# Two float32 projections of a streaming encoder's cross attention, written as split products

## The chip, the cores and the metric

The kernel runs on one core of a Trainium2 chip. The metric is the device time of one execution in microseconds, as the median over several runs. TensorE (PE in the profile) multiplies, VectorE (DVE) and ScalarE (ACT) do the elementwise work, GpSimd (POOL) and SyncE (SP) issue transfers.

## What is computed

One inference step of a two-layer encoder for 512 prompt frames and 32 sample frames, 544 columns in all, with 1024 features. Each layer has a mixer sub-layer with three branches, a cross attention into 256 memory tokens, and a SwiGLU FFN, each between a norm before and a norm behind. The part that matters here:

```python
def _rmsnorm(x, g):
    x32 = x.astype(jnp.float32)
    y = x32 * lax.rsqrt(jnp.mean(x32 * x32, axis=-1, keepdims=True) + RMS_EPS)
    return (y * g.astype(jnp.float32)).astype(x.dtype)
...
def _cross_attention(h, mem_k, mem_v, w_xq, w_xo):
    b, t, _ = h.shape
    q = (h @ w_xq).reshape(b, t, XATTN_HEADS, XATTN_HEAD_DIM)
    s = jnp.einsum('bqhd,bkhd->bhqk', q, mem_k).astype(jnp.float32) * XATTN_HEAD_DIM ** -0.5
    p = jax.nn.softmax(s, axis=-1)
    o = jnp.einsum('bhqk,bkhd->bqhd', p.astype(mem_v.dtype), mem_v).reshape(b, t, XATTN_W)
    return o @ w_xo
...
    x = x + _rmsnorm(y, norm_mix_post)
    x = x + _rmsnorm(_cross_attention(_rmsnorm(x, norm_x_pre), mem_k, mem_v, w_xq, w_xo), norm_x_post)
    x = x + _rmsnorm(_swiglu(_rmsnorm(x, norm_ffn_pre), w_ffn_in, w_ffn_out), norm_ffn_post)
```

`w_xq` is 1024 x 512, `w_xo` is 512 x 1024, all in float32.

## The kernel before

The residual `xT` and the normalised input `hT` stay on chip, features on the partitions, as 8 tiles of 128 x 544. A dense product makes one output tile of 128 features at a time: for each of its 8 (or 4) input tiles, one weight tile of 128 x 128 stands against two halves of 272 columns. There are two ways to do it:

- `dense` (line 716) multiplies in float32 straight from the weight ring. One matmul of it shows as two records in the profile.
- `dense_split` (line 726) takes weight and input each as a high and a low part in the type fp32r and sums three products: high x high, high x low, low x high. VectorE splits the weights in `split_unit` (line 1867): a cast of the ring slot into `WHI` (line 1865 of the helper `take_high`) and a subtraction into `WLO` (line 1875). Both have two places, taken in turn, so a tile can be split once the tile two before it has been multiplied. The input is split once, in `prenorm_split` (line 1834): two `scalar_tensor_tensor` for a pair of tiles, a drain, a cast, a drain, a subtraction that adds one to `x_split`.

Before the change all dense products of the layers are split but those of the memory keys and values (`w_xkv`, line 1258), the queries (`w_xq`) and the attention output (`w_xo`), both of them line 722.

The weights come through `ring`, four slots of 8 x 128 columns, filled by SyncE in the order of use (`unit`, line 447). Each load waits until the slot's last user is done: for a split tile that is its split (`split_done`), for a float32 tile the product itself (`tile_done`). Two ring slots serve two memory tiles, so the slots of the first two `w_xq` tiles come free when the sixth of the eight memory tiles is done:

```python
                for j in range(8):
                    unit("w_xkv", 0, 8, P * j, tiles(G_MEM + 2 * (j // 2) + 2))
                for j in range(4):
                    unit("w_xq", 0, 8, P * j, tiles(G_XQ + j + 1))
```

Nothing is scheduled by a planner: each engine has its program written out in order, and semaphores tie them. On VectorE the order around the change is: the last evacuations of the mixer's output product; `postnorm` (adds the mixer's result to `xT`, which lets ScalarE square it and TensorE sum it); a wait for `rstd_ready`, the reciprocal norm; `prenorm` (line 1828, writes `hT`); one scaled copy for each query tile; the barrier `phase_end`; attention; the sum of the squares of the output tiles (`add_square`, line 1819), which TensorE's `norm_added` takes; the first two FFN splits; the next norm. TensorE goes meanwhile through the memory products, the query product, attention (scores, transposed probabilities, values for 17 tiles, four heads), and the output product. In attention VectorE takes the maximum, the reciprocal and the scaling of each tile, and at four points (`x_evac`, after tiles 8, 12, 16 and at the end) it copies one head's 128 x 512 result from PSUM into `OX`; the 32 sample columns are one small copy at tile 4. ScalarE does the exponentials and copies the transposed probabilities.

## Time and profile before

| | |
|---|---|
| median of 3 runs | 2880.22 us (2878.37 to 2882.38) |
| the profiled execution | 2874.14 us, span 2872.3 us |
| granted TensorE clock, mean | 0.991 |
| TensorE busy | 2750.8 us (96%) |
| VectorE busy | 1611.0 us (56%) |
| ScalarE busy | 753.7 us (26%) |
| GpSimd busy | 244.2 us (9%) |
| DMA engines' share taken by the main queue | 28.7% |

Busy time is the time in which an engine had an instruction under way; it does not say that the end depended on it. The chain of work that ended last does: it is followed back from the last instruction, at each step to what released it. A timeline has one line for a run of like instructions, with the start, the length, and in brackets how long the engine was idle before it and what ended that. The granted clock is 1.00 at 2.4 GHz and 0.50 at 1.2 GHz.

### The profile page before, as it was taken

What the parts mean: (1) busy time and instruction counts of PE and PEld (TensorE: products, weight loads), DVE (VectorE), ACT (ScalarE), POOL (GpSimd) and SP (SyncE); (2) the same over time, 40 slices, a digit from 0 to 9 for tenths busy, and PEclk for the clock granted to TensorE, in tenths of its full rate; (3) what the DMA queues carried; (4) which work ended last, traced back from release to release, by engine and by line L of the source; (5) the groups of instructions that cost most, each with busy time, mean ns of one, the idle gap of its engine ahead of it and who ended that gap; (6) DMA issues with size and microseconds to landing.
All of it is one profiled execution on the core that took longest, in us unless ns stands there. A gap on an engine that the chain in (4) does not pass through costs nothing.

```text
span 2872.3 us, 63037 instructions
## 1 busy us (share of the span) xinstructions
PE 2750.8 (96%) x26472; PEld 2571.1 (90%) x26472; DVE 1611.0 (56%) x2967; ACT 753.7 (26%) x1803; POOL 244.2 (9%) x423
## 2 busy tenths in 40 slices
PE   7999999999999989999989999999999998999998
PEld 6877889999999789999988778899999996999997
DVE  5444665666664266664374455556666533766633
ACT  1143343333332330000112433433223324200001
POOL 1221112000000100000001211110000000000000
PEclk9999999999999999999999999999999999999999
DMA  4453436222263133333234434452224532233231
GB/s 136 127 144 105 144 107 170 72 72 65 82 173 100 46 89 89 89 87 88 77 90 132 120 111 139 103 160 72 72 68 115 153 92 73 71 89 89 85 88 58
DMA packets 420762, 290.26 MB, mean 101 GB/s; under 512 B 38544, under 2 KB 386352, under 8 KB 420352
## 3 DMA queue, kind: packets, MB, share of 16 engines
q1 hardware_dynamic: 398496, 228.64, 28.7%
q0 software_dynamic: 21984, 57.59, 6.3%
q8 instruction: 210, 3.44, 0.5%
q14 instruction: 72, 0.59, 0.1%
HBM read 232.12 MB, written 54.07 MB: 100 GB/s over the span
## 4 chain that ended last, share of the span: by engine, by line
PE 80%; DVE 8%; ACT 3%; DVEq 3%; DMA 2%; issue 2%; ACTq 0%; SPq 0%
PE PS L744 35%; PE PS L813 10%; PE PS L1116 8%; PE PS L1049 7%; PE PS L722 4%; PE PS L1258 2%; DMA U<-gate_scratch 2%; ACT U L1373 1%; PE PS L859 1%; PE PS L1090 1%; ACT U L1376 1%; PE PS L895 1%; PE PS L763 1%; PE PS L974 1%; PE PS L1194 1%
## 5 line engine op out<-in xcount | busy, mean ns | idle before, releaser
L744 PE MATMUL PS<-U_r,WHI 128*128 128x272 f32 x2656 | 474.4, 289 | 12.5 <-DVEq L2285 9.0
L1376 ACT COPY U<-PS 128x272 f32<-128x272 f32 (+9 forms) x782 | 273.1, 373 | 728.3 <-PE PS L1116 139.8
L1865 DVE CAST WHI<-ring 128x1024 fp32r<-128x1024 f32 (+1 forms) x240 | 164.1, 684 | 473.3 <-PE PS L744 365.3
L744 PEld LDWEIGHTS PS<-U_r,WHI 128*128 128x128 f32 x2656 | 386.1, 188 | 18.1 <-DVEq L2285 13.2
L744 PE MATMUL PS<-brT_r,WHI 128*128 128x272 f32 x1728 | 357.3, 288 | 1.4 <-DVEq L1876 1.4
L744 PE MATMUL PS<-U_r,WLO 128*128 128x272 f32 x1696 | 350.0, 288 | 0.0
L744 PE MATMUL PS<-hT_r,WHI 128*128 128x272 f32 x1696 | 349.7, 288 | 0.0
L1875 DVE TENSOR_TENSOR WLO<-ring,WHI 128x1024 fp32r<-128x1024 f32 (+1 forms) x240 | 289.7, 1207 | 19.4 <-issue 1.3
L744 PE MATMUL PS<-brT_r,WLO 128*128 128x272 f32 x1344 | 278.2, 288 | 0.0
L744 PEld LDWEIGHTS PS<-brT_r,WHI 128*128 128x128 f32 x1728 | 271.5, 188 | 2.2 <-DVEq L1876 2.2
L813 PE MATMUL PS<-U_r,WHI 128*128 128x272 f32 x832 | 261.6, 314 | 12.2 <-ACT U L1376 12.0
L744 PEld LDWEIGHTS PS<-hT_r,WHI 128*128 128x128 f32 x1696 | 266.5, 189 | 0.0
L744 PEld LDWEIGHTS PS<-U_r,WLO 128*128 128x128 f32 x1696 | 265.6, 188 | 0.0
L813 PE MATMUL PS<-U_r,WLO 128*128 128x272 f32 x832 | 242.1, 291 | 0.0
L813 PE MATMUL PS<-hT_r,WHI 128*128 128x272 f32 x832 | 241.0, 290 | 0.0
L1049 PE MATMUL PS<-U_r,WHI 128*128 128x272 f32 x768 | 229.7, 299 | 2.8 <-DVEq L2080 2.4
L1049 PE MATMUL PS<-U_r,WLO 128*128 128x272 f32 x768 | 221.8, 289 | 0.0
L1049 PE MATMUL PS<-hT_r,WHI 128*128 128x272 f32 x768 | 220.9, 288 | 0.0
L1116 PE MATMUL PS<-U 64*64 64x64 f32 (+1 forms) x5184 | 213.2, 238 | 0.0
L744 PEld LDWEIGHTS PS<-brT_r,WLO 128*128 128x128 f32 x1344 | 209.8, 189 | 0.0
L1116 PEld LDWEIGHTS PS<-U 64*64 64x64 f32 x5184 | 207.2, 134 | 1.3
L813 PEld LDWEIGHTS PS<-U_r,WHI 128*128 128x128 f32 x832 | 158.7, 191 | 31.5 <-issue 15.0
(336 smaller groups left out, 4291.5 us busy)
## 6 DMA issues: line engine op xcount, KB each, us to landing
ring<-in_w_in_dram SPq DMA_DIRECT2D x126, 512.0 KB, 4.3
ring<-in_w_ffn_in_dram SPq DMA_DIRECT2D x88, 512.0 KB, 3.8
ring<-in_w_ffn_out_dram SPq DMA_DIRECT2D x32, 448.0 KB, 3.7
proj_scratch<-U POOLq DMA_DIRECT2D x104, 136.0 KB, 2.1
U<-proj_scratch SPq DMA_DIRECT2D x48, 272.0 KB, 4.2
ring<-in_w_branch_dram SPq DMA_DIRECT2D x48, 256.0 KB, 3.2
gate_scratch<-U POOLq DMA_DIRECT2D x88, 136.0 KB, 3.2
U<-gate_scratch SPq DMA_DIRECT2D x44, 272.0 KB, 2.9
```

The costliest lines, as they stand in the source:

```text
L722: ins = mm(PS[0:width, 2 * q + h, 0:HT], ring[:, n % RING, k, 0:width], rhs(k, h), start=(k == 0), stop=(k == kn - 1))
L744: ins = mm(PS[:, 2 * q + h, 0:HT], w, half(x, h), start=(first and k == 0 and n == 0), stop=(last and k == kn - 1 and n == len(terms) - 1))
L763: ins = mm(PS[:, 2 * j + h, 0:HT], w, half(x, h), start=(k == 0 and n == 0), stop=(k == KM - 1 and n == 2))
L813: ins = mm(PS[:, 7, 0:HT], w, half(x, h), start=(k == 0 and i == 0), stop=(k == 7 and i == 2))
L859: mm(PS[:, b, 0:n], q, FK[it % 2][0:66, h, 0:n], start=True, stop=False)
L895: ins = mm(PS[o, 6, i * P:(i + 1) * P], FVT[it % 2][:, h, t, :], pt[:, t * P:(t + 1) * P], start=(t == 0), stop=(t == i))
L1049: ins = mm(PS[:, 6 + h, 0:HT], w, half(x, h), start=(k == 0 and i == 0), stop=(k == 7 and i == 2))
L1116: ins = mm(PS[r, bank, cols], w_c[r], x_c[r], start=(n == 0), stop=(n == len(pairs) - 1))
L1258: ins = mm(PS[:, 2 + n % 4, u * P:(u + 1) * P], MNT[:, k, t * P:(t + 1) * P], ring[:, (U_MEM + 2 * s + u) % RING, k, :], start=(k == 0), s ...
L1376: return act.copy(out, in_)
L1865: copy(hi, src)
L1875: tt(lo, w, hi.bitcast(F32), ALU.subtract)
```

## The change

The query and the output product become split products. In detail:

- The tables of split tiles get four entries for `w_xq` (`V_XQ`, 95) and eight for `w_xo` (`V_XO`, 99); the FFN's numbers move up by 12. The ring's order and its unit numbers stay.
- `prenorm` of the query's input becomes `prenorm_split`, with the high part in a new buffer `XH` and the low part in `hT`'s place. TensorE starts its first query tile pair by pair as `x_split` rises, where it waited for all of `hT` before.
- VectorE splits the query's first two weight tiles between `postnorm` and `prenorm_split`, the third and the fourth behind the first and the second product; the first two tiles of `w_xo` at the start of attention, the others in the output product.
- `x_evac` and the copy of the sample columns each become a cast into `OXH` and, after a drain, a subtraction into `OXL`.
- The additions of squares and the first two FFN splits now lie between the output product's splits, one tile behind the other.
- SyncE's loads for slots that `w_xq` and `w_xo` have used wait for the split and not for the product.

```diff
-V_LATE, V_GATE, V_BR, V_OUT, V_FFI, V_FFO = 13, 39, 63, 87, 95, 139
+V_LATE, V_GATE, V_BR, V_OUT, V_XQ, V_XO, V_FFI, V_FFO = 13, 39, 63, 87, 95, 99, 107, 151
...
@@ -52,17 +52,17 @@
 IN_PAIR = (0, 1, 3, 2, 0, 1, 2, 0, 1, 2, 0, 2, 1)
 IN_ROT = (4, 4, 4, 4, 4, 4, 3, 3, 3, 3, 3, 2, 4)
 SPLITS = V_FFO + 8 * len(FFO_SPLIT)
-X_SPLITS = 4 + 6 + 8
+X_SPLITS = 4 + 6 + 4 + 8
 
 
 def unit_of(v):
 
-    return v if v < V_FFI else v + U_FFI - V_FFI
+    return v if v < V_XQ else v + U_XQ - V_XQ
 
 
 def depth_of(v):
 
-    if V_BR <= v < V_OUT:
+    if V_BR <= v < V_OUT or V_XO <= v < V_FFI:
         return 4
     return FFO_SPLIT[(v - V_FFO) % 3] if v >= V_FFO else 8
 
@@ -329,6 +329,7 @@
         BH = cv(12, T, of=UR)
         MNT = cv(KM, N_MEM)
         SQ1 = cv(KM, T)
+        XH = carver(2 * KM * T + T + 6 * T + 12 * T + KM * N_MEM)(KM, T, of=UR)
         YH = carver(0)(KM, T, of=UR)
 
         cv = carver(KM * T + T)
@@ -339,6 +340,8 @@
         OX = cv(X_HEADS, T)
         XP, XPT = cv(3, N_MEM), cv(2, 2 * P)
         XST = cv(3, 4)
+        OXH = cv(X_HEADS, T, of=UR)
+        OXL = carver(KM * T + T + 2 * 512 * 4 + 2 * X_HEADS * N_MEM + X_HEADS * T)(X_HEADS, T, of=UR)
 
         cv = carver(0)
         GH, GL = cv(KF, T, of=UR), cv(KF, T, of=UR)
@@ -615,9 +618,9 @@
                 for j in range(8):
                     unit("w_xkv", 0, 8, P * j, tiles(G_MEM + 2 * (j // 2) + 2))
                 for j in range(4):
-                    unit("w_xq", 0, 8, P * j, tiles(G_XQ + j + 1))
+                    unit("w_xq", 0, 8, P * j, split(V_XQ + j))
                 for j in range(8):
-                    unit("w_xo", 0, 4, P * j, tiles(G_XO + j + 1))
+                    unit("w_xo", 0, 4, P * j, split(V_XO + j))
                 for j in range(11):
                     for m in range(4):
                         unit("w_ffn_in", 0, 8, (m // 2) * FFN + 256 * j + P * (m % 2), split(V_FFI + 4 * j + m))
@@ -1263,9 +1266,9 @@
                     if s == 1:
                         group_sums(l, 2, 0)
                         group_sums(l, 2, KM // 2)
-                pe.wait_ge(h_ready, l * 24 + 16)
                 for n in range(N_XQ):
-                    dense(l, G_XQ + n, n % 4, U_XQ + n, 8, of_h, rot=3)
+                    dense_split(l, G_XQ + n, n % 4, V_XQ + n, lambda k: (XH[:, k, :], hTR[:, k, :]), rot=3,
+                                need=10 if n == 0 else None)
                 phase_end(pe, l, 2)
                 pe.wait_ge(xa_loaded, (l + 1) * 32)
 
@@ -1325,7 +1328,7 @@
                         x_values(k - 3)
                 pe.wait_ge(xa_evac, l * 5 + 5)
                 for n in range(N_XO):
-                    dense(l, G_XO + n, n % 3, U_XO + n, 4, lambda k, h: half(OX[:, k, :], h), rot=3)
+                    dense_split(l, G_XO + n, n % 3, V_XO + n, lambda k: (OXH[:, k, :], OXL[:, k, :]), rot=3)
                 norm_added(l, 3)
 
 
@@ -1336,7 +1339,7 @@
                 def of_f(k):
                     return HF[:, k, :], hTR[:, k, :]
 
-                dense_first(l, G_FFI, V_FFI, of_f, 10, sums=4)
+                dense_first(l, G_FFI, V_FFI, of_f, 14, sums=4)
                 sums_spread(l, 4)
                 ffn_in(0, 2, 1)
                 pe.wait_ge(rstd_ready, l * 6 + 5)
@@ -2322,16 +2325,25 @@
                         if 1 <= n - 2 <= KM - 3:
                             add_square(l, 1, n - 2)
                 postnorm(l, 1, "norm_mix_post")
-                prenorm(l, 2, "norm_x_pre")
+                split_unit(l, V_XQ)
+                split_unit(l, V_XQ + 1)
+                prenorm_split(l, 2, "norm_x_pre", XH)
                 for n in range(N_XQ):
                     tile(l, G_XQ + n)
+                    if n < N_XQ - 2:
+                        split_unit(l, V_XQ + n + 2)
                     ts(half(QX[:, n, :], 1), PS[:, 2 * (n % 4) + 1, 0:HT], X_DIM ** -0.5, None, ALU.mult) \
                         .then_inc(tile_freed_dve, 1)
                 phase_end(dve, l, 2)
+                split_unit(l, V_XO)
+                split_unit(l, V_XO + 1)
 
                 def x_evac(h):
                     dve.wait_ge(xa_out, l * 5 + h + 2)
-                    copy(OX[:, h, 0:SEQ], PS[:, x_bank(h), :]).then_inc(xa_evac, 1)
+                    take_high(OXH[:, h, 0:SEQ], PS[:, x_bank(h), :])
+                    dve.drain()
+                    tt(OXL[:, h, 0:SEQ], PS[:, x_bank(h), :], OXH[:, h, 0:SEQ].bitcast(F32), ALU.subtract) \
+                        .then_inc(xa_evac, 1)
 
                 for k in range(N_XT + 1):
                     if k < N_XT:
@@ -2347,16 +2359,19 @@
                             .then_inc(xa_norm, 1)
                     if k == 4:
                         dve.wait_ge(xa_out, l * 5 + 1)
-                        copy(OX[:, :, SEQ:T], PS[:, 7, 0:4 * DEC_SEQ].rearrange("p (h n) -> p h n", h=4)) \
-                            .then_inc(xa_evac, 1)
+                        rows = PS[:, 7, 0:4 * DEC_SEQ].rearrange("p (h n) -> p h n", h=4)
+                        take_high(OXH[:, :, SEQ:T], rows)
+                        dve.drain()
+                        tt(OXL[:, :, SEQ:T], rows, OXH[:, :, SEQ:T].bitcast(F32), ALU.subtract).then_inc(xa_evac, 1)
                     if k in (8, 12, 16):
                         x_evac((k - 8) // 4)
                 x_evac(3)
                 dve.sem_inc(tile_freed_dve, N_XO)
-                for a in range(1, KM - 2):
-                    add_square(l, 3, a)
-                split_unit(l, V_FFI)
-                split_unit(l, V_FFI + 1)
+                for n in range(N_XO):
+                    tile(l, G_XO + n)
+                    split_unit(l, V_XO + n + 2)
+                    if 1 <= n - 1 <= KM - 3:
+                        add_square(l, 3, n - 1)
                 dve.wait_ge(rstd_ready, l * 6 + 4)
 
                 def updated(b):
```

How VectorE's instructions move, between the post-norm and attention (in `prenorm` and its successor; `hT` is the normalised input, `VT` the gains, `U` the pool in which `XH` lies, `U_r` and `hT_r` the same memory as fp32r). Before:

```order
L1858 SCALAR_TENSOR_TENSOR hT<-hT,VT,U 128x544 x2
L1855 TENSOR_TENSOR xT<-xT,hT 128x544 x2
L1832 SCALAR_TENSOR_TENSOR hT<-xT,VT,U 128x544 [waits rstd_ready]
L1832 SCALAR_TENSOR_TENSOR hT<-xT,VT,U 128x544 x7
L2328 TENSOR_SCALAR U<-PS 128x272 [waits tile_done] x4
L2339 TENSOR_REDUCE U<-PS 128x1 [waits xa_scores,phase_ended]
```

and with the change:

```order
L1861 SCALAR_TENSOR_TENSOR hT<-hT,VT,U 128x544 x2
L1858 TENSOR_TENSOR xT<-xT,hT 128x544 x2
L1868 CAST WHI<-ring 128x1024 [waits slot_loaded3]
L1878 TENSOR_TENSOR WLO<-ring,WHI 128x1024
L1868 CAST WHI<-ring 128x1024 [waits slot_loaded0]
L1878 TENSOR_TENSOR WLO<-ring,WHI 128x1024
L1842 SCALAR_TENSOR_TENSOR hT<-xT,VT,U 128x544 [waits rstd_ready]
L1842 SCALAR_TENSOR_TENSOR hT<-xT,VT,U 128x544
L1868 CAST U_r<-hT 128x1088
L1847 TENSOR_TENSOR hT_r<-hT,U_r 128x1088
L1842 SCALAR_TENSOR_TENSOR hT<-xT,VT,U 128x544 x2
L1868 CAST U_r<-hT 128x1088
```

Two splits, each behind the arrival of its ring slot, now stand between the last instruction of the post-norm and the first that waits for the reciprocal norm.

The second place is VectorE from the end of attention to the norm behind it. Before:

```order
L2344 RECIPROCAL U<-U 128x1 [waits xa_exp]
L2346 TENSOR_SCALAR U<-U 128x256
L2334 COPY U<-PS 128x512 [waits xa_out]
L1822 TENSOR_TENSOR U<-U 128x544 [waits sq_act] x5
L1865 CAST WHI<-ring 128x1024 [waits slot_loaded3]
L1875 TENSOR_TENSOR WLO<-ring,WHI 128x1024
L1865 CAST WHI<-ring 128x1024 [waits slot_loaded0]
L1875 TENSOR_TENSOR WLO<-ring,WHI 128x1024
L2363 SCALAR_TENSOR_TENSOR hT<-hT,VT,U 128x544 [waits rstd_ready]
```

and with the change (the splits of `w_xo` are the ones of 512 columns; five more of them, with four additions of squares, stand between the two pieces shown):

```order
L2356 RECIPROCAL U<-U 128x1 [waits xa_exp]
L2358 TENSOR_SCALAR U<-U 128x256
L1868 CAST U_r<-PS 128x512 [waits xa_out]
L2345 TENSOR_TENSOR U_r<-PS,U_r 128x512
L1868 CAST WHI<-ring 128x512 [waits slot_loaded1,tile_done]
L1878 TENSOR_TENSOR WLO<-ring,WHI 128x512
```

```order
L1825 TENSOR_TENSOR U<-U 128x544 [waits sq_act]
L1868 CAST WHI<-ring 128x1024 [waits slot_loaded3,tile_done]
L1878 TENSOR_TENSOR WLO<-ring,WHI 128x1024
L1825 TENSOR_TENSOR U<-U 128x544 [waits sq_act]
L1868 CAST WHI<-ring 128x1024 [waits slot_loaded0,tile_done]
L1878 TENSOR_TENSOR WLO<-ring,WHI 128x1024
L2378 SCALAR_TENSOR_TENSOR hT<-hT,VT,U 128x544 [waits rstd_ready]
```

The copy of a head is now two instructions, and the additions of squares, which had the output product to themselves, each stand behind a split that waits for its tile.

## Rows read from the trace of the kernel before

**Rows 1.** The page, the chain that ended last: by engine, then by line.

```profile
PE 80%; DVE 8%; ACT 3%; DVEq 3%; DMA 2%; issue 2%; ACTq 0%; SPq 0%
PE PS L744 35%; PE PS L813 10%; PE PS L1116 8%; PE PS L1049 7%; PE PS L722 4%; PE PS L1258 2%; DMA U<-gate_scratch 2%; ACT U L1373 1%; PE PS L859 1%; PE PS L1090 1%; ACT U L1376 1%; PE PS L895 1%; PE PS L763 1%; PE PS L974 1%; PE PS L1194 1%
```

**Rows 2.** Timeline of PE, first layer: start us, us, engine, line, op, out<-in, count.

```profile
913.63 10.88 PE L1258 MATMUL PS<-ring,U 128*128 128x128 f32 x96
924.35 29.50 PE L722 MATMUL PS<-hT,ring 128*128 128x272 f32 x128
985.63 29.60 PE L722 MATMUL PS<-U,ring 128*128 128x272 f32 x128 [0.78 <-DVE U L2334]
```

**Rows 3.** Timeline of DVE, same stretch; idle before and releaser in brackets.

```profile
915.49 5.66 DVE L1832 SCALAR_TENSOR_TENSOR hT<-xT,VT,U 128x544 f32<-128x544 f32 x8 [9.56 <-ACTq L1411]
931.89 0.44 DVE L2328 TENSOR_SCALAR U<-PS 128x272 f32<-128x272 f32 x1 [10.75 <-PE PS L722]
953.89 0.44 DVE L2328 TENSOR_SCALAR U<-PS 128x272 f32<-128x272 f32 x1 [6.89 <-PE PS L722]
...
959.14 0.95 DVE L2339 TENSOR_REDUCE U<-PS 128x1 f32<-128x256 f32 x2 [4.81 <-PE PS L1288]
```

**Rows 4.** SP's timeline in both layers; then landing of the first and second load.

```profile
917.40 8.14 SPq L458 DMA_DIRECT2D ring<-in_w_xq_dram  x4
...
2337.62 8.14 SPq L458 DMA_DIRECT2D ring<-in_w_xq_dram  x4
...
DMA to landing us min/median/max: 3.8/3.8/3.8
...
DMA to landing us min/median/max: 5.0/5.0/5.0
```

**Rows 5.** Timeline of DVE: two weight tiles of depth 8 split back to back.

```profile
1010.04 0.69 DVE L1865 CAST WHI<-ring 128x1024 fp32r<-128x1024 f32 x1
1012.14 0.69 DVE L1865 CAST WHI<-ring 128x1024 fp32r<-128x1024 f32 x1
```

**Rows 6.** Timeline of DVE: the normalised input split in pairs, start of layer 2.

```profile
1458.74 0.73 DVE L1865 CAST U_r<-hT 128x1088 fp32r<-128x1088 f32 x1
1460.75 1.47 DVE L1839 SCALAR_TENSOR_TENSOR hT<-xT,VT,U 128x544 f32<-128x544 f32 x2
1462.32 0.73 DVE L1865 CAST U_r<-hT 128x1088 fp32r<-128x1088 f32 x1
1466.27 0.69 DVE L1865 CAST WHI<-ring 128x1024 fp32r<-128x1024 f32 x1 [1.86 <-PE PS L763]
```

**Rows 7.** Timeline of PE: the matmuls that wait for the last pair there.

```profile
1464.46 0.52 PE L763 MATMUL PS<-U_r,WHI 128*128 128x272 f32 x2
```

**Rows 8.** Timeline of DVE: two splits that each wait for a split-product tile.

```profile
1092.29 0.69 DVE L1865 CAST WHI<-ring 128x1024 fp32r<-128x1024 f32 x1 [3.12 <-PE PS L744]
1098.30 0.69 DVE L1865 CAST WHI<-ring 128x1024 fp32r<-128x1024 f32 x1 [3.11 <-PE PS L744]
```

**Rows 9.** Windows of PE: stretch, us, busy (x), granted clock, DMA share, GB/s.

```profile
1023.60:1026.60 3.00, 2.98 (x13) 0.50 0.02 5
1432.00:1436.70 4.70, 0.14 (x2) 0.95 0.00 0
1436.70:1440.00 3.30, 3.25 (x8) 0.55 0.00 0
2444.20:2449.70 5.50, 5.50 (x24) 0.50 0.01 3
```

**Rows 10.** The chain of waits through the first layer's attention tiles.

```profile
971.16 0.60 DVE U L2334
984.89 0.70 DVE U L2334
```

**Rows 11.** Groups of DVE instructions by form, 600 to 860 us: busy, mean ns.

```profile
L2284 DVE TENSOR_TENSOR WLO<-ring,WHI 128x512 fp32r<-128x512 f32 x22 | 15.2, 690 | 13.6 <-ACT WHI L1376 13.6
L2226 DVE COPY U<-PS 128x384 f32<-128x384 f32 x6 | 3.3, 558 | 4.7 <-PE PS L1116 4.7
```

## The prediction

> **What bounds the kernel now.** I read the chain that ended last first: TensorE holds 80% of it, and most lines in it are split products that the change does not touch; the plain float32 products of line 722 are 4% and the memory products of line 1258 are 2% [rows 1]. So what the change can move is small, and it is read from the one stretch between the mixer and the FFN, which both layers pass alike. The timelines of TensorE and VectorE there show four things. The memory products run until 924.35 and the query product follows without a gap; it takes 29.50 us, and the output product takes 29.60 us [rows 2]. VectorE idles 9.56 us for the reciprocal norm once the post-norm is over, from 905.93, and normalises from 915.49 for 5.66 us, so it is done before TensorE wants it [rows 3]. In between, attention goes tile by tile through all three engines. Last, the timeline of the load queue: the first two `w_xq` tiles are issued only at 917.40 [rows 4]. They go into ring slots that the memory products of `w_xkv` hold until their sixth tile is done, and that is the row to keep in mind.
>
> **Cheaper matmuls (the gain).** A float32 tile of 16 matmuls takes (953.89 - 931.89) / 3 = 7.33 us [rows 3]. A split tile of the same size, 48 matmuls, takes 1098.30 - 1092.29 = 6.01 us [rows 8], or 0.125 us a matmul. The output product has eight tiles of half that depth: 8 x (7.33 - 6.01) / 2 = 5.3 us less. The query product has four tiles; the last three save 3 x 1.32 = 4.0 us. The first is told below.
>
> **A rule on this term.** In the rows a split tile costs 6.01 / 7.33 = 0.82 of a float32 tile [rows 3, 8]. The Trainium skill (FP8 and Floating Point Precision, TensorE Precision Notes) says that true FP32 takes four passes through the array. By that three products at a pass each would cost 0.75; the trace does not agree with that ratio here, and what it would make of the time is a rival below.
>
> **The two splits ahead of the pre-norm (the price).** VectorE works in order. It now reaches the split of the first query tile at 905.93, and that split waits for its ring slot. The loads are issued at 917.40, and from issue to landing the first takes 3.8 us and the second, issued right behind, 5.0 us [rows 4]. Nothing in the change releases those slots sooner: they wait for memory tiles whose code is the same. So the first split starts at 917.40 + 3.8 = 921.2. One split takes 1012.14 - 1010.04 = 2.10 us [rows 5], and the second load has landed by about 922.9, before the first split ends at 923.3. Both end at 925.4. The wait for the reciprocal norm ended at 915.49, so the pre-norm starts 9.9 us late, and the idle time that was to hide the splits has passed before they can begin. Queued behind the waiting split on VectorE are the pre-norm and the halves of the input; TensorE waits for these.
>
> **The pre-norm itself is longer.** The start of the second layer shows the same helper: one pair of tiles comes every 1462.32 - 1458.74 = 3.58 us, and from the start of the last pair's first instruction to the matmuls that wait for it are 1464.46 - 1460.75 = 3.71 us [rows 6, 7]. Here the four pairs release TensorE at 929.1, 932.7, 936.3 and 925.4 + 3 x 3.58 + 3.71 = 939.9. A tile's share of a pair is 12 matmuls, 1.5 us, so TensorE is starved throughout. From the release of the last pair until VectorE sees the first tile done are 1466.27 - 1464.46 = 1.8 us there, and as many matmuls lie in between [rows 6, 7]. So the first query tile is seen done at 941.7 instead of 931.89 [rows 3]: 9.8 us later. With the 4.0 us saved behind it, the query product ends **5.8 us later** in each layer. The two other query splits (2.1 us each) lie beside tiles of 6.01 us and cost nothing.
>
> **The clock.** TensorE will be idle from 924.35 to 929.1, 4.75 us, and after that works 1.5 us of each 3.58. The trace has such a case: of the 4.70 us before 1436.7 it was busy 0.14 us, and in the stretch behind it the granted clock was 0.55; behind the waits ahead of the FFN it is 0.50 (the lower of its two levels, 1.2 GHz) for 3.0 us in one layer and for 5.5 us in the other, at 3.00 / 13 = 0.23 us a matmul [rows 9]. A slow clock costs nothing while pairs are awaited (12 x 0.23 = 2.8 us, under 3.58), but it does once the last pair is there. I take 12 x (0.23 - 0.125) = 1.3 us a layer; the bounds are 0 and half of the longest stretch, 2.75 us. The Trainium skill (TensorE: Matmul & The Clock Gate, HAM oscillation) describes short bursts of matmuls between waits that each start on the throttled clock. By that the upper bound would be nearer.
>
> **Attention.** `x_evac` becomes a cast from PSUM and a subtraction from PSUM with a drain between. The copy it replaces takes 0.60 us of the chain [rows 10], and the cast should match it. The subtraction: 0.69 us for 128x512 between SBUF tiles, and a PSUM copy of 384 columns takes 0.56, so PSUM is no dearer [rows 11]. With the drain I take 0.77 us for each of the four heads. The chain holds this copy at heads 0 and 1 and at head 3 (the first and the last of the three: [rows 10]), so there it counts in full, 2.3 us. At head 2 it delays the last normalisation, which has a few tenths of slack: 0.5 us. The small one for the 32 sample rows (about 0.35 us more) has slack in the next tile. Sum **2.8 us**; bounds 0.75 (only the last head counts, the engines catch up elsewhere) and 3.4 (all of it). The two output splits of depth 4 come first in this stage, while VectorE idles 4.81 us until its first score at 959.14 [rows 3]; a cast of 0.42 and a subtraction of 0.69 with drains are 1.3 us, twice that is 2.6, so they are hidden. In the output product VectorE has for each tile a split (1.3) and an addition of 544 columns (by the 0.69 for 512 some 0.8 with its drain), 2.1 us beside 3.0; with the depth-8 split of the FFN's first tile it is 2.10 + 0.8 = 2.9 beside 3.0, so I give 0.1 us to the sum of squares behind the last tile. The FFN splits were hidden before and are now.
>
> **The sum.** For each layer: +5.8 (query) + 1.3 (clock) + 2.8 (attention) - 5.3 (output) + 0.1 = +4.7 us, and twice that is **+9.4 us**. Against the profiled execution (2874.14 us, span 2872.3) that is 2883.5. The median of the runs shown is 6.1 us above that execution, so the forecast for the median is 2880.2 + 9.4 = **2889.6 us**, 0.33% slower. About 0.2%, 5.8 us, is what a measurement of this kernel can tell from no change.
>
> **Rivals.** *Attention absorbs it and the clock stays up:* 5.8 + 0.75 - 5.3 = +1.3 a layer, +2.5 us, 2882.7, no change to be told. For it speaks that the three engines each have idle time in a tile; against it, that the copies stand on the chain by name. Chance 0.17.
> *The splits are hidden after all (faster):* the two loads are in the ring before VectorE has to start splitting, at 915.49 - 4.2 = 911.3. Then the last pair is released at 915.5 + 14.5 = 930.0, the first tile is seen at 931.8, as before, and a layer changes by -4.0 + 2.8 - 5.3 = -6.5 us, -13 us in all, 2867. It decides at 911.3 for the second load's landing; the row says 922.9 and the issue itself is at 917.40 [rows 4], so it needs slots that come free 11 us sooner. Chance 0.04.
> *A split matmul costs a quarter of a float32 one:* a split tile is then 7.33 x 0.75 = 5.5 us, which takes 2.0 us more from the output product and 1.5 us more from the three query tiles, 3.5 a layer: +2.4 us in all, 2882.6. The 6.01 us of a split tile [rows 8] is TensorE back to back, each with VectorE waiting 3.1 us for it, so 0.03. That rule is the one of the Trainium skill named above (FP8 and Floating Point Precision).
> *Every bound at its dear end:* +5.8 + 2.75 + 3.4 + 0.3 - 5.3 = +6.95 a layer, +13.9 us, 2894.1; chance 0.16, the same sign as the forecast. The forecast itself has 0.60. That the change does not do what it says I leave at nothing: the order of instructions shows every edit in place.
>
> **How the numbers follow.** The range takes in the second rival's neighbours on the low side and the dear end on the high side, with two microseconds for the measurement at each: 2881 to 2896. Slower by over 0.2%: the forecast and the dear end, 0.76, less a little for the forecast without a slow clock (+6.8 us, close to the limit): 0.74. Within 0.2%: 0.17 + 0.03 + 0.02 = 0.22. Faster: 0.04.
>
> **What would show it.** In the profile of the changed kernel VectorE's first query split starts near 921 with some 15 us of idle before it, put down to the load; the pre-norm starts near 925.4; TensorE is idle some 4.7 us between the memory and the query products; the first query tile ends near 941.7 and the last near 959.7; the granted clock between 929 and 943 is under 1. From the first score to the output product attention is 2.8 us longer, and the output product takes 24.2 us. A first query split that starts before 916 would make the prediction wrong, and so would attention that grows by less than a microsecond, or an output product above 27 us.

## The result, and the profile after

The change makes the kernel slower: 2887.40 us as the median of 12 runs (2883.54 to 2893.13), against 2877.67 us of the kernel before in as many (2872.56 to 2882.72). The ratio is 1.0035, with a 95% interval of 1.0025 to 1.0045, or +9.7 us. The forecast was +9.4 us; its 2889.6 us stood on the 2880.22 us of the three runs known then.

The execution that was profiled is the slowest of the twelve: 2893.13 us, span 2891.2, mean granted clock 0.984, against 2874.14, 2872.3 and 0.991 of the profile before. So sizes of single terms are taken from stretches that both profiles have, and the whole from the runs.

First the page's summary of the chain that ended last, to be read against [rows 1]:

```profile
PE 79%; DVE 9%; DVEq 3%; ACT 3%; DMA 2%; issue 2%; ACTq 0%; SPq 0%
PE PS L747 38%; PE PS L816 10%; PE PS L1119 8%; PE PS L1052 7%; DMA U<-gate_scratch 2%; PE PS L1261 1%; PE PS L862 1%; PE PS L1093 1%; ACT U L1376 1%; ACT U L1379 1%; PE PS L766 1%; PE PS L898 1%; DVE WLO L1878 1%; PE PS L977 1%; PE PS L1197 1%
```

TensorE's share is a point lower and VectorE's a point higher, and the float32 line of the two products (L722 before, 4%) is gone from the list; its work is now in the split products of L747. Nothing in it tells where the time went; the timelines do. SyncE and then VectorE in the first layer, to be read against [rows 3, 4]:

```profile
920.22 8.14 SPq L461 DMA_DIRECT2D ring<-in_w_xq_dram  x4
```

```profile
924.32 0.69 DVE L1868 CAST WHI<-ring 128x1024 fp32r<-128x1024 f32 x1 [15.57 <-DMA ring<-in_w_xq_dram]
...
926.44 0.70 DVE L1868 CAST WHI<-ring 128x1024 fp32r<-128x1024 f32 x1
...
928.55 1.48 DVE L1842 SCALAR_TENSOR_TENSOR hT<-xT,VT,U 128x544 f32<-128x544 f32 x2
...
939.29 1.47 DVE L1842 SCALAR_TENSOR_TENSOR hT<-xT,VT,U 128x544 f32<-128x544 f32 x2
...
945.57 0.69 DVE L1868 CAST WHI<-ring 128x1024 fp32r<-128x1024 f32 x1 [2.63 <-PE PS L747]
...
964.39 0.44 DVE L2335 TENSOR_SCALAR U<-PS 128x272 f32<-128x272 f32 x1 [5.58 <-PE PS L747]
```

The `w_xq` loads are issued 3.76 us behind the start of the last memory products, as before (the whole program is 2.8 us later here). VectorE has nothing to do for 15.57 us, and the releaser named is the transfer of `w_xq`. At 924.32, 4.1 us behind the issue, the first split begins; the second follows at 926.44; the pre-norm begins at 928.55, in front of which the norm had long been ready. The last of its pairs begins at 939.29, the first query tile is seen done at 945.57, and the last query copy starts at 964.39. TensorE in the same time:

```profile
916.46 10.88 PE L1261 MATMUL PS<-ring,U 128*128 128x128 f32 x96
932.36 0.79 PE L747 MATMUL PS<-U_r,WHI 128*128 128x272 f32 x2 [5.02 <-DVE hT_r L1847]
...
943.00 0.52 PE L747 MATMUL PS<-U_r,WHI 128*128 128x272 f32 x2 [1.81 <-DVE hT_r L1847]
...
999.87 0.77 PE L747 MATMUL PS<-U_r,WHI 128*128 128x272 f32 x4 [1.55 <-DVE U_r L2345]
```

Between the end of the memory products and the first pair it is idle 5.02 us, and 1.81 us before the last pair. The granted clock of these stretches (stretch, us, busy, granted clock, DMA share, GB/s):

```profile
932.90:936.50 3.60, 3.17 (x15) 0.50 0.35 83
936.50:940.20 3.70, 2.35 (x17) 0.95 0.00 0
940.20:943.00 2.80, 0.99 (x8) 1.00 0.00 0
943.00:946.00 3.00, 3.00 (x15) 0.62 0.02 5
946.00:949.00 3.00, 3.00 (x22) 0.81 0.06 19
949.00:955.00 6.00, 6.00 (x50) 1.00 0.12 35
```

It is at the lower level for the first pair, back at 1.00 by the third, and falls again just as the last pair is released: 943 to 947 runs at 0.23 us a matmul. Last the chain of waits where a head is evacuated, for [rows 10]:

```profile
982.74 0.60 DVEq L2344
983.34 0.07 issue
983.41 0.69 DVE U_r L2345
...
998.36 0.69 DVE U_r L1868
...
999.13 0.70 DVE U_r L2345
...
999.87 3.13 PE PS L747 x23
```

Where one copy of 0.60 us stood there are now the cast and its drain (0.60), a gap of 0.07 and the subtraction (0.69), 1.36 us in all; at the last head 1.51 us instead of 0.73 lie between attention and the output product.

This table gives the two layers' stretch in every profile, in us behind the start of the last memory products (the row at 913.63 before): the start of the last query copy, the start of the output product, and the start of the first instruction of the norm behind it. The last column is the sum over both layers against the kernel before. Each row is one execution, so it shows where time goes; how much a kernel gains or loses is told by its runs.

| kernel | first layer: query, output, norm | second layer: query, output, norm | both, against before |
|---|---|---|---|
| before | 40.3, 72.0, 106.0 | 40.2, 72.3, 106.4 |  |
| the change | 47.9, 83.4, 112.4 | 47.8, 84.7, 115.2 | +15.1 |
| the change, second profile (e8) | 46.3, 83.2, 113.7 | 46.2, 80.5, 111.0 | +12.3 |
| query product only (e1) | 46.2, 78.0, 112.0 | 46.2, 79.0, 113.1 | +12.7 |
| output product only (e2) | 40.2, 74.6, 103.6 | 40.2, 74.7, 105.2 | -3.6 |
| splits between the pairs (e3) | 38.7, 74.2, 103.2 | 38.7, 73.1, 103.5 | -5.8 |
| early loads (e4) | 36.2, 70.5, 99.5 | 36.2, 73.2, 103.6 | -9.4 |
| idle time filled (e5) | 46.2, 83.2, 113.6 | 46.4, 80.7, 111.3 | +12.4 |
| spread evacuations (e6) | 46.4, 79.6, 108.6 | 46.4, 80.8, 109.8 | +5.9 |
| early loads and spread (e7) | 36.2, 69.4, 98.4 | 36.2, 69.4, 98.4 | -15.6 |
| early output start (e11) | 46.4, 79.0, 108.0 | 46.2, 79.9, 108.8 | +4.4 |
| all three (e12) | 36.2, 68.8, 97.7 | 36.2, 68.8, 97.8 | -16.9 |

So the stretch is 6.3 us longer in the first layer and 8.8 in the second, 15.1 of the 18.9 us by which the two spans differ. Of the rest, 2.8 us lie ahead of the first layer's stretch and 0.9 us behind the two stretches, in code that the change does not touch.

### The profile page after: what moved, and what is told of

Read it like the earlier page. It is cut to its first block, busy times and chain, and to the rows that moved or that the text cites. A ratio compares the mean times of both kernels' runs of the same rounds, so it can differ in the third digit from the quotient of the medians.

```text
span 2891.2 us, 63717 instructions
## 1 busy us (share of the span) xinstructions
PE 2748.3 (95%) x26728; PEld 2585.1 (89%) x26728; DVE 1667.7 (58%) x3041; ACT 752.6 (26%) x1803; POOL 244.3 (8%) x423
## 4 chain that ended last, share of the span: by engine, by line
PE 79%; DVE 9%; DVEq 3%; ACT 3%; DMA 2%; issue 2%; ACTq 0%; SPq 0%
PE PS L747 38%; PE PS L816 10%; PE PS L1119 8%; PE PS L1052 7%; DMA U<-gate_scratch 2%; PE PS L1261 1%; PE PS L862 1%; PE PS L1093 1%; ACT U L1376 1%; ACT U L1379 1%; PE PS L766 1%; PE PS L898 1%; DVE WLO L1878 1%; PE PS L977 1%; PE PS L1197 1%
## 5 line engine op out<-in xcount | busy, mean ns | idle before, releaser
L747 PE MATMUL PS<-U_r,WHI 128*128 128x272 f32 x3040 | 548.4, 291 | 33.3 <-DVE hT_r L1847 17.3
L1868 DVE CAST WHI<-ring 128x1024 fp32r<-128x1024 f32 (+2 forms) x264 | 177.0, 670 | 539.8 <-PE PS L747 402.1
L747 PEld LDWEIGHTS PS<-U_r,WHI 128*128 128x128 f32 x3040 | 445.9, 190 | 41.1 <-DVEq L2288 13.6
L747 PE MATMUL PS<-U_r,WLO 128*128 128x272 f32 x1952 | 405.5, 289 | 0.0
L747 PE MATMUL PS<-hT_r,WHI 128*128 128x272 f32 x1824 | 378.5, 289 | 0.0
L747 PE MATMUL PS<-brT_r,WHI 128*128 128x272 f32 x1728 | 357.3, 288 | 1.0 <-DVEq L1879 1.0
L1878 DVE TENSOR_TENSOR WLO<-ring,WHI 128x1024 fp32r<-128x1024 f32 (+2 forms) x264 | 310.7, 1177 | 21.2 <-issue 1.3
L747 PEld LDWEIGHTS PS<-U_r,WLO 128*128 128x128 f32 x1952 | 308.6, 190 | 0.0
L747 PEld LDWEIGHTS PS<-hT_r,WHI 128*128 128x128 f32 x1824 | 289.2, 190 | 0.0
L747 PE MATMUL PS<-brT_r,WLO 128*128 128x272 f32 x1344 | 278.2, 288 | 0.0
L816 PE MATMUL PS<-U_r,WHI 128*128 128x272 f32 x832 | 262.7, 316 | 12.2 <-ACT U L1379 12.0
L747 PEld LDWEIGHTS PS<-brT_r,WHI 128*128 128x128 f32 x1728 | 271.5, 188 | 1.9 <-DVEq L1879 1.9
L816 PE MATMUL PS<-U_r,WLO 128*128 128x272 f32 x832 | 243.5, 293 | 0.0
L816 PE MATMUL PS<-hT_r,WHI 128*128 128x272 f32 x832 | 242.3, 291 | 0.0
L1052 PE MATMUL PS<-U_r,WHI 128*128 128x272 f32 x768 | 229.7, 299 | 3.2 <-DVEq L2083 2.4
L1052 PE MATMUL PS<-U_r,WLO 128*128 128x272 f32 x768 | 221.9, 289 | 0.0
L1052 PE MATMUL PS<-hT_r,WHI 128*128 128x272 f32 x768 | 220.9, 288 | 0.0
L747 PEld LDWEIGHTS PS<-brT_r,WLO 128*128 128x128 f32 x1344 | 209.8, 189 | 0.0
L816 PEld LDWEIGHTS PS<-U_r,WHI 128*128 128x128 f32 x832 | 159.8, 192 | 31.5 <-issue 15.0
```

Of the source, the lines that this page charges most:

```text
L747: ins = mm(PS[:, 2 * q + h, 0:HT], w, half(x, h), start=(first and k == 0 and n == 0), stop=(last and k == kn - 1 and n == len(terms) - 1))
L816: ins = mm(PS[:, 7, 0:HT], w, half(x, h), start=(k == 0 and i == 0), stop=(k == 7 and i == 2))
L1052: ins = mm(PS[:, 6 + h, 0:HT], w, half(x, h), start=(k == 0 and i == 0), stop=(k == 7 and i == 2))
L1868: copy(hi, src)
L1878: tt(lo, w, hi.bitcast(F32), ALU.subtract)
```

## The experiments

Theory (the forecast's): the two query weights arrive only behind the wait they were to be split in, so the pre-norm and all behind it start late; the evacuations add to attention; the slow clock adds to both; the cheaper matmuls give back about half. Rivals: the evacuations are the price and the query side is even; the longer pre-norm is the price and not the order of the splits; the clock costs nothing. Every kernel was timed beside the kernel before, in 5 to 12 runs. "Against the change" means against its +9.7 us, unless another figure is named; a second timing of it, below, gave +12.2.

**Each product alone.** In the first, the output product, its evacuations and the order behind them are as before the change:

```diff
-                    unit("w_xo", 0, 4, P * j, split(V_XO + j))
+                    unit("w_xo", 0, 4, P * j, tiles(G_XO + j + 1))
...
-                    dense_split(l, G_XO + n, n % 3, V_XO + n, lambda k: (OXH[:, k, :], OXL[:, k, :]), rot=3)
+                    dense(l, G_XO + n, n % 3, U_XO + n, 4, lambda k, h: half(OX[:, k, :], h), rot=3)
```

> Only the query product is a split product; the output product, x_evac and their order are as before the change. Late weights (the forecast): the query side alone carries the loss, +5.8 us a layer and 1 to 2.5 us for the slow clock, so +14 to +17 us over before, slower than the whole change by about 4 us. Rival, the loss lies in attention and the output product and the query product is about even: within 3 us of before.

Measured: 2886.54 us against 2877.43, ratio 1.0031 (1.0018 to 1.0043), +9 us. The sign and the side are as the forecast has them, the size is not: +14 to +17 was too much, and this kernel is not slower than the whole change, as had been expected. The profile shows why. The last query copy comes 6.0 and 5.9 us later than before, no more, although the granted clock is low for the first pairs here too. The slow clock had been counted in and cost nothing. The stretch as a whole is 12.7 us longer in this profile, the runs say +9; the interval reaches to 12.4. That execution as a whole is only 8.5 us longer than the one profiled before (spans 2880.8 and 2872.3), because the code between the two stretches takes 1310.7 us in it and took 1314.2 before; why, no run shows.

In the second, the query product and its pre-norm are as before:

```diff
-                unit("w_xq", 0, 8, P * j, split(V_XQ + j))
+                unit("w_xq", 0, 8, P * j, tiles(G_XQ + j + 1))
...
-                split_unit(l, V_XQ)
-                split_unit(l, V_XQ + 1)
-                prenorm_split(l, 2, "norm_x_pre", XH)
+                prenorm(l, 2, "norm_x_pre")
```

> Only the output product is a split product; the query product and its pre-norm are as before the change. Forecast: attention +2.8 to +3.7 us a layer, output product -5.3, so -3 to -5 us against before. Rival, the evacuations cost more than the output product gives back: +2 us or more. Rival, attention absorbs them: -9 us.

Measured: 2870.74 us, ratio 0.9980 (0.9971 to 0.9988), -6.7 us; somewhat better than expected. In its profile attention is 34.3 and 34.5 us where it was 31.7 and 32.1, so +2.6 and +2.4, and the output product with the norm's first wait is 29.0 us in the first layer and 30.5 in the second, where it was 34.0 in both. The first is the forecast's -5.2 nearly to the tenth (-5.1). The second is 1.5 us short of it, and these rows of the second layer show what is missing:

```profile
2403.19 1.34 PE L1317 MATMUL PS<-U 128*128 128x128 f32 x8
2406.07 0.82 PE L747 MATMUL PS<-U_r,WHI 128*128 128x272 f32 x4 [1.55 <-DVE U_r L2341]
```

```profile
2406.00:2409.00 3.00, 2.92 (x15) 0.61 0.00 0
2409.00:2412.00 3.00, 3.00 (x22) 0.82 0.00 0
```

TensorE has been idle 1.55 us for the last head's evacuation, and the output product then starts at a granted clock of 0.61. The kernel before has an idle time of 0.78 us there [rows 2], and its profile shows a clock of 1.00 in both layers.

The two halves do not add up to the whole: +9.1 and -6.7 us make +2.4, where the change has +9.7 and, in its second timing, +12.2. In the profiles the stretches add up to 12.7 - 3.6 = +9.1 us, against 15.1 and 12.3; what is missing there is slow clock, in other places in each execution (see the clock below). The rest of the gap lies outside the stretch and is not explained. So the output half pays when it is made alone, and the query half carries the loss, but their prices in the whole are known only as far as the stretches show them.

**The order of the splits.** Here the first query split stands between the second and the third pair of the pre-norm, and the second behind the last:

```diff
                 for a in range(0, KM, 2):
+                    if between is not None and a == 4:
+                        split_unit(l, between)
...
-                split_unit(l, V_XQ)
-                split_unit(l, V_XQ + 1)
-                prenorm_split(l, 2, "norm_x_pre", XH)
+                prenorm_split(l, 2, "norm_x_pre", XH, between=V_XQ)
+                split_unit(l, V_XQ + 1)
```

> The whole change, but the first query split stands between the second and the third pair of the split pre-norm and the second behind the last pair, so the pre-norm starts when the reciprocal norm is ready. Late weights: the first query tile is seen done about 2 us later than before the change instead of 10 to 11, the last one 1.6 us earlier; -7 us against before, about -17 against the change. Rival, the longer pre-norm itself is the price (3.58 us a pair instead of 1.4) and the order of the splits does not matter: within 3 us of the change, +8 to +10 over before.

Measured: 2871.37 us, ratio 0.9977 (0.9967 to 0.9986), -6.1 us against before and some 16 against the change. VectorE's timeline:

```profile
915.12 1.48 DVE L1844 SCALAR_TENSOR_TENSOR hT<-xT,VT,U 128x544 f32<-128x544 f32 x2 [9.55 <-ACTq L1414]
...
922.27 0.69 DVE L1870 CAST WHI<-ring 128x1024 fp32r<-128x1024 f32 x1
...
951.97 0.44 DVE L2336 TENSOR_SCALAR U<-PS 128x272 f32<-128x272 f32 x1 [5.58 <-PE PS L747]
```

The pre-norm starts 9.55 us behind the post-norm, at once with the reciprocal norm; the split at 922.27 finds its load there. The last query copy is 38.7 us into the stretch, 1.6 us before the 40.3 of the kernel before, as expected. The longer pre-norm, which this kernel has in full, is not the price; it is the waiting splits ahead of it.

**The loads themselves.** The order of the change is kept, but the first two `w_xq` tiles come out of the ring and into a buffer of their own as soon as the branch products are done:

```diff
+                sp.wait_ge(tile_done, l * TILES + G_BR + N_BR)
+                for j in range(2):
+                    load(XQW[:, j, :, :], A["w_xq"][ds(l, 1)].rearrange("l (k p) n -> p (l k) n", p=P)
+                         [:, :, P * j:P * j + P]).then_inc(xq_early, 16)
...
-                for j in range(4):
+                for j in range(2, 4):
                     unit("w_xq", 0, 8, P * j, split(V_XQ + j))
...
```

> The whole change in its own order, but the first two query weight tiles are loaded into a buffer of their own once the branch products are done, so they are there when VectorE comes to split them. Late weights: the splits lie in the wait for the reciprocal norm as meant, the pre-norm starts with it, TensorE has no gap behind the memory products; -12 us against before, about -22 against the change. Rival, something else than the load holds the pre-norm: no change against the whole change.

Measured: 2865.18 us, ratio 0.9958 (0.9947 to 0.9969), -12.3 us against before and 22 against the change.

```profile
906.26 0.69 DVE L1874 CAST WHI<-U 128x1024 fp32r<-128x1024 f32 x1
...
908.37 0.69 DVE L1874 CAST WHI<-U 128x1024 fp32r<-128x1024 f32 x1
...
915.73 1.48 DVE L1848 SCALAR_TENSOR_TENSOR hT<-xT,VT,U 128x544 f32<-128x544 f32 x2 [5.36 <-ACTq L1420]
...
950.04 0.44 DVE L2348 TENSOR_SCALAR U<-PS 128x272 f32<-128x272 f32 x1 [5.58 <-PE PS L753]
```

Both splits now stand at 906.26 and 908.37, directly behind the post-norm and inside the wait for the reciprocal norm; 5.36 us of it are still idle. The last query copy is 36.2 us into the stretch in both layers, 4.1 us ahead of the kernel before. The edit has one side effect: with two tiles fewer in the ring, the loads behind them are issued earlier too (the third and the fourth `w_xq` tile at 917.64). But in the change no split of the query and output products behind the first two waits for its load; the next one waits for TensorE (the row at 945.57 above). So the late arrival of the first two weight tiles is shown to be what makes the change slow.

**The clock in the query product.** TensorE fills its idle time around the first query tile with matmuls that nobody reads (`fill` is 3 for that tile and 0 for the others):

```diff
+                pe.wait_ge(rstd_ready, l * 6 + 3)
+                for i in range(9):
+                    mm(PS[:, 6, 0:HT], ones[:, :], half(RS, 0), start=True, stop=True)
...
+                    if fill and k in (2, 4, 6):
+                        for i in range(fill):
+                            mm(PS[:, 6, 0:HT], ones[:, :], half(RS, 0), start=True, stop=True)
```

> The whole change, and TensorE fills its idle time around the first query tile with float32 matmuls whose result nobody reads (9 ahead of the tile, 3 ahead of each later pair, into a PSUM bank that is free). They add no wait. The clock theory: the granted clock stays at 1.00 through the query product, the last query copy is seen 46.2 us behind the start of the last memory products instead of 47.9 (before: 40.3), so -3 to -4 us against the change in both layers together. Rival, the slow clock costs nothing because VectorE's pairs set the pace: no difference, or slower if the extra matmuls hold up the first pair.

It is read beside the change itself, timed at the same time on the same chip:

> The change once more, on the same chip as the three beside it, so that they can be compared with it at the same time: +8 to +12 us over before. The query product's stretch and the second layer's output product should again show slow-clock stretches; their places in attention may differ.

Measured: 2886.30 us (1.0034, 1.0022 to 1.0047) with the filling and 2889.50 us (1.0050, 1.0036 to 1.0063) without; the intervals overlap, so the runs leave open whether the 3.2 us between the medians are real. The windows of the filled kernel and then of the change, each from the first pair to the second tile:

```profile
928.00:931.50 3.50, 2.85 (x18) 1.00 0.95 230
931.50:935.00 3.50, 3.14 (x19) 1.00 0.00 0
935.00:938.50 3.50, 3.07 (x19) 1.00 0.02 5
938.50:942.00 3.50, 3.06 (x22) 1.00 0.00 0
```

```profile
929.00:932.50 3.50, 1.44 (x6) 0.66 1.19 303
932.50:936.00 3.50, 3.07 (x14) 0.50 0.10 23
936.00:939.50 3.50, 2.78 (x19) 0.86 0.00 0
939.50:943.00 3.50, 1.69 (x14) 1.00 0.00 0
943.00:946.00 3.00, 3.00 (x26) 1.00 0.02 5
```

The filling does hold the clock at 1.00, where the change has 0.66, 0.50 and 0.86. And yet the last query copy stands at 46.2 and 46.4 us with it and at 46.3 and 46.2 without. While VectorE's pairs set the pace, a slow clock is hidden behind them, and in this execution it is back before the last pair. The forecast's 1.3 us were not there. In the change's first profile they were (47.9 and 47.8): the clock fell a second time, at 943. So this cost exists, but in one of the five profiled executions that have this order of splits and no filling.

The change's second profile (e8) tells where the slow clock is paid instead:

```profile
966.00:972.00 6.00, 5.08 (x33) 0.93 0.53 139
972.00:978.00 6.00, 6.00 (x24) 0.50 0.04 6
978.00:984.00 6.00, 5.31 (x33) 1.00 0.20 25
996.00:1001.00 5.00, 3.44 (x18) 0.74 0.00 0
1001.00:1005.00 4.00, 4.00 (x31) 0.90 0.00 0
```

From 972 to 978, in the first attention tiles, it is 0.50, and TensorE is busy all the time: attention lasts 37.0 us in this layer and 34.4 in the other. At the start of the output product it is 0.74 and then 0.90, with 30.4 and 30.5 us instead of 29.0. The filled kernel, whose clock was at 1.00 all through the query product, has the same two costs: 37.0 us of attention in its first layer, and 30.3 and 30.5 us behind the start of the output product.

**The evacuations.** The subtraction of heads 0 to 2 moves one attention tile back (`x_high` is the cast and the drain of `x_evac`, `x_low` its subtraction):

```diff
                     if k in (8, 12, 16):
-                        x_evac((k - 8) // 4)
-                x_evac(3)
+                        x_high((k - 8) // 4)
+                    if k in (9, 13, 17):
+                        x_low((k - 9) // 4)
+                x_high(3)
+                x_low(3)
```

> The whole change, but of each head's evacuation the cast is done at its tile and the subtraction one attention tile later, for heads 0 to 2. If VectorE's idle time of some 0.4 us in each attention tile absorbs the half that is moved, attention is 1 to 1.5 us shorter a layer than with the change, -2 to -3 us. If attention is bound by VectorE's total work, nothing changes.

Measured: 2884.97 us, ratio 1.0027 (1.0016 to 1.0038); against 1.0050 of the change beside it, 4.5 us less, though the intervals touch. In the profile attention is 33.2 us in the layer with the clock at 1.00, 1.1 less than the 34.35 of the change with a full clock. The three subtractions that are moved are 3 x 0.69 = 2.1 us of work, so VectorE's idle time takes up about half of them and the rest stays on the chain. That is 2.3 us for both layers. The output product also starts at a full clock in both layers here (29.0 us where the change beside it has 30.4 and 30.5).

**The idle time ahead of the output product.** TensorE begins with the first three heads and asks for the fourth at its fourth input tile:

```diff
-                pe.wait_ge(xa_evac, l * 5 + 5)
                 for n in range(N_XO):
-                    dense_split(l, G_XO + n, n % 3, V_XO + n, lambda k: (OXH[:, k, :], OXL[:, k, :]), rot=3)
+                    dense_split(l, G_XO + n, n % 3, V_XO + n, lambda k: (OXH[:, k, :], OXL[:, k, :]), rot=3,
+                                ready=(xa_evac, l * 5 + 1) if n == 0 else None)
...
-                x_evac(3)
                 dve.sem_inc(tile_freed_dve, N_XO)
+                x_evac(3)
```

> The whole change, but TensorE starts the output product with the first three heads and waits for the fourth head's parts only at its fourth input tile. It takes away the 1.55 us in which TensorE stands idle between attention and the output product; 2.25 us of matmuls cover VectorE's last cast and subtraction. If only the idle time counts: -1.5 us a layer, -3 us against the change. If that idle time is also what sends the clock down at the start of the output product (two of three layers seen so far with it), the output product is 29.0 us from its start to the norm's first instruction in both layers and another 1 us a layer goes, -5 us against the change.

Measured: 2881.64 us, ratio 1.0013 (1.0004 to 1.0022), +3.6 us over before and so some 6 us less than the change (8.6 by its second timing). This is the larger of the two expectations (-5), or more. From the output product's start to the norm behind it are 29.0 and 28.9 us:

```profile
993.94 0.44 PE PS L1301 x2
994.38 0.45 PE PS L1317 x4
994.84 0.71 PE PS L1317 x4
995.56 4.53 PE PS L747 x36
```

The output product (L747) follows the last attention matmuls with nothing between. Over all profiles the start of a split output product is told apart like this: with the whole evacuation and the wait in front of it, 8 of 12 took 30.3 us or more; with the spread evacuation or the early start, all 8 took 28.9 to 29.0. The idle time alone does not decide it: the kernels with the spread evacuation keep the wait of 1.55 us, and start at full clock in all four of their layers. These are the rows of the kernel with early loads and spread evacuations (e7, below), first layer, the timeline and then the stretch with its granted clock:

```profile
980.60 0.77 PE L753 MATMUL PS<-U_r,WHI 128*128 128x272 f32 x4 [1.55 <-DVE U_r L2360]
```

```profile
980.50:983.50 3.00, 2.90 (x23) 1.00 0.00 0
```

**What beats both.** Early loads and spread evacuations in one kernel:

> Early loads of the first two query tiles and the spread evacuations together. Both theories add: -12 us (early loads) and -2 to -3 us (spread) against before, so -14 to -15 us, about -24 against the change. If the spread is worth nothing, as the early loads alone.

Measured: 2861.87 us, ratio 0.9946 (0.9934 to 0.9959), -15.4 us. And with the early start of the output product as well:

> Early loads, spread evacuations and the early start of the output product together. Early loads and spread gave 0.9946 of before; with -1.5 us a layer more: -18 to -19 us against before, ratio 0.9935.

Measured: 2857.79 us against 2878.05, ratio 0.9927 (0.9915 to 0.9940), -20.3 us, and some 30 us faster than the change. Both kernels are made of the edits above and of nothing else. The second one's last query copy, output product and norm stand at 36.2, 68.8 and 97.7 or 97.8 us in both layers.

## Why the prediction was right

- **Late weights: as forecast.** The forecast had the first split 3.8 us behind the issue, the pre-norm 9.9 us late, TensorE idle 4.75 us and the last query copy 5.8 us later. In the profile after they are 4.1 us, 10.2 us (928.55 less the program's shift of 2.8, against 915.49), 5.02 us, and 5.9 to 6.2 us in the ten layers of the kernels that have the order of the change and a clock that recovers in time (e1, e5, e6, e8, e11). That nothing frees the slots sooner was the step it all hung on, and the early loads show it from the other side: -4.1 us, where the rival with hidden splits had -4.0.
- **Attention: +2.8 forecast, +2.6 and +2.4 measured** by the output product alone. The sum was right, its parts less so. Heads 0 and 1 were put down with 0.77 us each and head 2 with 0.5; the first evacuations are 988.68 - 982.66 = 6.02 us apart, where they were 5.46, so 0.56 each, and the way from the third to the fourth (994.70 to 998.36) and from the fourth to the output product are 0.8 us longer each. The slack was at the first two heads and not at the third. That PSUM is no dearer for the subtraction was read from a shorter copy, which does not show it; the profile after does, with 0.69 us.
- **Output product: -5.2 forecast (-5.3 and the 0.1 for the sum of squares), -5.1 measured** at a full clock. A split tile takes 6.02 us here too (958.37 to 964.39 are the starts of the last two query copies), 0.82 of a float32 tile. The rival of a quarter for each split matmul falls. The Trainium skill (FP8 and Floating Point Precision, TensorE Precision Notes) says that true FP32 takes four passes; with one pass for each product of a split, which that section does not state, the estimate would be 0.75, and the trace with its 0.82 does not agree.
- **The clock: the size nearly right, its place wrong.** The step that failed is "I take 12 x (0.23 - 0.125) = 1.3 us a layer" behind the last query pair. Filling the idle time there moved the last query copy by nothing. Slow stretches cost 0 in the query product in most layers (1.7 in both layers of one execution), but 1.1 to 2.7 us in attention where they fall there, and 1.4 to 1.5 at the start of most output products. In the second profile of the change this is 2.6 + 1.45 + 1.55 = 5.6 us for both layers, where the forecast had 2.6. That the total of the runs came out within a microsecond of the forecast is thus partly luck: the terms without the clock sum to 2 x (6.0 - 5.1) + 2.6 + 2.4 = +6.8 us, and what the runs add to that varies from one execution to the next. The Trainium skill (TensorE: Matmul & The Clock Gate, HAM oscillation) describes bursts between waits that run throttled again and again; the trace agrees that it happens, and shows that it costs nothing as long as another engine's pace is slower still.
- **What stays open:** why the clock falls in attention in one layer and not in another. In the change's second profile the idle times of TensorE from the end of the query product to the fall are the same in the layer with the fall and the one without, and no kernel was made for it. Over all twelve profiles attention has a slow stretch, beginning 8 to 12 us behind the last query copy, in 11 of the 20 layers with a split query product, and in none of the 4 with a float32 one (the kernel before and e2), which is too few to name the query product as the cause. Early loads, spread evacuations and filled idle time do not rule it out: e4, e5, e6 and e12 all have it.

## What to carry to other kernels

Work put into a wait needs its inputs there when the wait begins: look up when the load it stands on is issued, and what frees the slot for it. An in-order engine does not skip an early instruction whose data is late, so a misplaced preparation delays everything behind it; here two splits of 4.2 us put the pre-norm back by 10 us and the last query copy from 36.2 to 46.2 us. And when a product is made cheaper in matmuls, count what it adds to the copies that stand between the engines, and let the product begin with the parts that are already there.

## What the runs showed of the hardware

The granted clock fell to its lower level in attention after TensorE had been busy 5.08 of 6 us (the row from 966.00 above, and 6.00 of 6 us busy at 0.50 behind it), and in 8 of 12 layers at the start of an output product behind an idle time of only 1.55 us; with the same 1.55 us and the evacuations spread it stayed at 1.00 in all four layers. The prediction had only looked for it behind the waits of about 5 us. And filling the idle time around the first query tile with matmuls kept the clock up there, at 1.00 in all four windows of the filled kernel, but not in the attention behind it.
